# Which engine copies the second prompt tile's dense expert weights out of PSUM

## The reference

```
h = RMSNorm(x);  proj = h @ w_in                       # two attention branches, gates
x = x + w_out(sigmoid(gA) * (oA @ w_br_a) + sigmoid(gB) * (oB @ w_br_b))
x = x + PEER(RMSNorm(x))

PEER: q = h @ w_pq;  s1, s2 = q halves against 128 keys each
      top-16 of each half, top-16 of their 256 sums, for each of 8 heads
      e = i1 * 128 + i2;  g = softmax(top sums)         # 128 experts a token, of 16384
      a = gelu(u[e] . h);   y = sum over the 128 experts of g * a * v[e]
```

## Time and profile before

| | |
|---|---|
| Time, median of 3 runs | 1579.57 us (1575.74 to 1583.34) |
| Profiled execution | 1577.69 us, its span 1575.9 us |
| PE busy | 1167.5 us, 74% |
| DVE busy | 1035.7 us, 66% |
| POOL busy | 646.8 us, 41% |
| ACT busy | 291.7 us, 19% |
| mean granted TensorE clock | 0.816 of 2.4 GHz |

### The profile page before, as it was taken

One profiled execution on the slowest core, in us unless ns is written; L12 is line 12 of the kernel. 1 busy time (PEld: TensorE's weight loads), 2 busy tenths in 40 slices (PEclk: granted clock), 3 DMA queues, 4 the chain that ended last, 5 costly groups with the idle time before them and its releaser, 6 DMA issues.

```text
span 1575.9 us, 12501 instructions
## 1 busy us (share of the span) xinstructions
PE 1167.5 (74%) x4129; PEld 695.2 (44%) x4129; DVE 1035.7 (66%) x2220; ACT 291.7 (19%) x701; POOL 646.8 (41%) x565
## 2 busy tenths in 40 slices
PE   7999998975420683674586584027799999999998
PEld 3444444852110673673244374026544444444443
DVE  2436313579999878777447569999856566666664
ACT  2024501210000011111046441149600000000000
POOL 1110000333333757767324453445544454444451
PEclk9999999997755555555698777556799999999999
DMA  7654231684643988998987765656699999999996
GB/s 265 219 187 164 81 143 44 250 293 161 250 140 97 358 275 325 364 339 282 389 296 250 253 228 202 228 175 208 233 409 410 409 410 409 409 409 410 409 401 252
DMA packets 155361, 434.92 MB, mean 276 GB/s; under 512 B 14592, under 2 KB 36496, under 8 KB 155040
## 3 DMA queue, kind: packets, MB, share of 16 engines
q0 software_dynamic: 74688, 271.66, 46.8%
q1 hardware_dynamic: 80608, 162.45, 28.3%
HBM read 427.72 MB, written 6.34 MB: 275 GB/s over the span
## 4 chain that ended last, share of the span: by engine, by line
PE 56%; DVE 21%; DMA 9%; ACT 8%; issue 3%; POOL 3%; SPq 1%; DVEq 0%; ACTq 0%
PE wide L1189 28%; DVE rows_ring L1505 6%; PE accumB L873 5%; PE accumA L873 4%; DMA ring<-in_w_in 3%; DMA rows_ring<-in_peer_u,expert 3%; ACT hot L805 3%; POOL rows_ring L576 2%; PE wide L1079 2%; PE accumB L1101 2%; PE accumB L1135 2%; PE transB L849 2%; PE transB L1135 2%; PE wide L952 2%; PE wide L991 2%
## 5 line engine op out<-in xcount | busy, mean ns | idle before, releaser
L576 POOL DMA_INDIRECT rows_ring<-in_peer_u,expert x384 | 477.9, 1245 | 437.8 <-DVE dots L1505 351.0
L1505 DVE CUSTOM_DVE_ANT_0 rows_ring<-rows_ring,arena 128x1024 f32<-128x1024 f32 x384 | 458.6, 1223 | 125.4 <-DMA rows_ring<-in_peer_u,expert 123.0
L1189 PE MATMUL wide<-ring,arena 128*128 128x512 f32 x1024 | 439.7, 592 | 0.7 <-issue 0.7
L1189 PEld LDWEIGHTS wide<-ring,arena 128*128 128x128 f32 x1024 | 194.5, 190 | 245.3 <-issue 245.3
L1510 DVE SCALAR_TENSOR_TENSOR x<-rows_ring,dots,x 128x1024 f32<-128x1024 f32 x128 | 164.4, 1284 | 99.2 <-DMA rows_ring<-in_peer_v,expert 99.2
L576 POOL DMA_INDIRECT rows_ring<-in_peer_v,expert x128 | 127.1, 993 | 136.1 <-DVE x L1510 129.1
L849 PE MATMUL transB<-ident,arena 128*128 128x128 f32 x198 | 48.7, 389 | 126.8 <-DVE arena L1290 59.8
L873 PE MATMUL accumB<-ring,arena 128*128 128x512 f32 (+1 forms) x192 | 89.1, 622 | 56.9 <-ACT arena L651 50.0
L849 PEld LDWEIGHTS transB<-ident,arena 128*128 128x128 f32 x198 | 31.5, 195 | 141.3 <-DVE arena L1290 60.6
L873 PE MATMUL accumB<-arena 128*128 128x512 f32 x160 | 74.4, 620 | 23.9 <-ACT arena L651 12.3
L873 PEld LDWEIGHTS accumB<-ring,arena 128*128 128x128 f32 x192 | 40.0, 212 | 103.5 <-ACT arena L651 52.4
(11 more groups left out here) (218 smaller groups left out, 1418.0 us busy)
## 6 DMA issues: line engine op xcount, KB each, us to landing
ring<-in_peer_v SPq DMA_DIRECT2D x128, 512.0 KB, 6.8
ring<-in_w_in SPq DMA_DIRECT2D x10, 2048.0 KB, 10.2
arena<-in_w_in SPq DMA_DIRECT2D x10, 2048.0 KB, 8.8
ring<-in_w_pq SPq DMA_DIRECT2D x4, 2048.0 KB, 9.9
arena<-in_w_pq SPq DMA_DIRECT2D x4, 2048.0 KB, 8.9
arena<-in_w_out SPq DMA_DIRECT2D x3, 2048.0 KB, 10.3
rows_ring<-in_peer_u,expert POOLq DMA_INDIRECT x384, 6.8
arena<-in_w_br_a SPq DMA_DIRECT2D x2, 2048.0 KB, 7.6
```

The costliest lines, as they stand in the source:

```text
L576: pool.indirect_dma_start(rowbuf[:, n % ROWS, :], None, u_rows if n < U_ROWS else v_rows, index).then_inc(S(f"rows{n % ROWS}"), 16)
L1189: ins = pe.matmul(wide[:, 2 * t + half, :], dense[t][:, b, :], vblock[:, b % VBLOCKS, half * 512:half * 512 + 512], start=b == 0, stop=b = ...
L1505: v.tensor_tensor_reduce(row, row, h2[:, t, :], 1.0, 0.0, ALU.mult, ALU.add, dots[:, t, k:k + 1]).then_inc(S("row_used"), 1)
```

## The change

For tile 1 (`t == 1`) the copy out of PSUM leaves ScalarE's list and goes into VectorE's. VectorE copies group k = n-1 after the `hot1` of group n, behind a wait for `built` of group k; after the last `hot1` it copies group 30 and then group 31. ScalarE's waits ahead of tile 1's first copy go to VectorE with it, where two are added: that the router's scores were copied, and that tile 0's 32 copies are done. Tile 0 is as before.

```diff
                         act.wait_ge(S("state_stored"), 16 * 10)
-                    elif g == 0:
-
-                        act.wait_ge(S("routed"), 12)
-                        act.wait_ge(S("row_used"), SAMPLE * SLOTS)
-                        act.wait_ge(to(G1, "score_done"), 4)
-                    if g:
+                    if g and t == 0:
                         put(g - 1)
-                put(TGROUPS - 1)
+                if t == 0:
+                    put(TGROUPS - 1)
...
                     signal(ins, "hot1_ready")
+                    if t == 0:
+                        continue
+                    if g == 0:
+
+                        v.wait_ge(S("routed"), 12)
+                        v.wait_ge(S("row_used"), SAMPLE * SLOTS)
+                        v.wait_ge(to(G1, "score_done"), 4)
+                        v.wait_ge(to(G1, "router_copied"), 4)
+                        v.wait_ge(S("dense_put"), TGROUPS)
+                    for k in [g - 1] * (g > 0) + [g] * (g == TGROUPS - 1):
+                        v.wait_ge(S("built"), TGROUPS + k + 1)
+                        signal(v.tensor_copy(dense[t][:, :, k * TOKENS:k * TOKENS + TOKENS],
+                                             built[(k + 1) % 2][:, :].rearrange("p (n b) -> p b n", n=TOKENS)),
+                               "dense_put")
```

## The result

The changed kernel takes 1587.07 us (median of 20 runs, 1582.28 to 1593.15), the kernel before 1581.40 beside it (20 runs). The ratio is 1.0042, 95% interval 1.0030 to 1.0055: 4.7 to 8.7 us slower. Timed a second time, on another occasion, it is 1.0047 (1.0024 to 1.0069). The forecast was 1592 in a range of 1582 to 1600, so direction and range hold; but 0.42% lies under the 0.5% that I had named as the bound of "no change", a band to which I gave a chance of 0.15 only. And the size is about half of the forecast: 6.6 us by the ratio (5.7 between the medians), where the sum had 14.1.

What follows compares the result with a forecast made beforehand. ScalarE bounds tile 1's weight building, whose last copy gates the closing pass. Moving the copies makes steps 12.37 us instead of 10.30, +14.1 us: 1577.69 + 14.1 = 1591.8, said as 1592, range 1582 to 1600.

Steps and rivals of the forecast that it cites:

- no change: Whole kernel: a time within about 0.5%, 7.9 us, of the kernel before; chance of "same" 0.15.
- the sum: Tile 1's weight building: step period 12.37 us against 10.30, last copy done at 1144.6 against 1130.49, +14.1 us.
- The bound and the pass: Closing PE pass: waits only for tile 1's last dense-weight copy, starts near 1144.7, keeps its 439.7 us.
- The price of the copy: Tile 1's VectorE copies out of PSUM, 128x512 f32: 0.60 us each, 2.40 us a step.
- C: Rival on tile 1's copies: 0.35 us each on VectorE with fast builds, -2.4 us, 1575.3; chance 0.05.
- D: Rival on tile 1's copies: the PSUM source's stride makes each 1.2 us, about +24 us, 1602; chance 0.10.
- First builds slow: Tile 1's steps: the first build of each takes 2.05 us on PE, after about 4.7 us of rest.
- rival A: Tile 1's steps: the first build of each stays fast, period 11.86 us, +10.5 us, 1588.2; chance 0.25.
- All later builds slow: Tile 1's steps: builds behind the first run slow too, two slow ones in a row ending 1.71 us apart.
- Rows and gathers: Gathers land in time; four more rows behind the pass's start cost 8.2 us, 2.05 each, within 12.64 us of cover.
- rival B: Tile 1's steps: all builds fast, VectorE alone sets 11.27 us a step, +4.3 us, 1582.0; chance 0.10.

Runs made afterwards that it cites:

- the doubled copy: Changed kernel with each VectorE copy done a second time behind a wait for the first: 1603.33 us, ratio to the kernel before 1.0158.
- The two kernels with extra products: Kernel before and changed kernel, each with unused PE products after tile 1's builds: 1575.11 us (ratio 0.9973) and 1582.49 us (1.0029 to the kernel before).

## Why the prediction was right, and where it was not

*The bound and the pass: right.* The pass follows the last copy (1137.78 + 0.69, pass at 1138.57) and kept its 439.72 us.

*The price of the copy: right.* 0.60 us added, 0.685 to 0.69 alone, as the two-input row from PSUM; a cost of the stride doesn't show. That row could not decide it, though: two-input instructions out of SBUF add 0.60 for 128x512 too, so it doesn't tell what a one-input copy loses by reading PSUM. With C and D out by the copies themselves, the doubled copy confirms that VectorE pays for them. The Trainium skill's rule (VectorE: DVE Perf Modes, "Why PSUM operands drop a tier"), one element a cycle for f32 out of PSUM, agrees with these rows: an SBUF copy of that size would have been about half as long by the earlier trace rows.

*First builds slow: right,* eight of eight in the first trace and 32 of 32 in all four (2.04 or 2.05 us), where five of eight took 1.13 to 1.20 us before; that is rival A out. That the stretch grew by just A's +10.5 and that the time lies nearest to A's 1588.2 is luck. In the changed kernel the granted clock falls during the rest ahead of a step, here between the builds of 1064.40 and 1070.27 (columns as in the earlier trace rows):

```profile
1066.00:1068.00 2.00, 0.00 (x0) 0.00 (x0) 2.00 (x5) 1.97 (x6) 1.70 (x2) 1.00 0.00 0
1069.00:1070.00 1.00, 0.00 (x0) 0.00 (x0) 1.00 (x6) 0.00 (x0) 0.95 (x1) 0.50 0.83 307
```

The two kernels with extra products bear this out: with PE's rest filled, the clock of the stretch is 0.96. The Trainium skill's rule (TensorE: Matmul & The Clock Gate, Part 1) that activity lifts the clock agrees with that, 0.71 to 0.96 here.

The prediction's reading of the kernel before was weaker than it looked. There the first builds of tile 1 don't sort by the rest ahead of them: beside the very first (15.43 us of rest), two take 2.05 and 2.08 us after 1.62 and 1.78 us of rest (at 1089.95 and 1110.38), and the five of 1.13 to 1.20 us come after 1.67 to 2.47. They sort by the clock granted just ahead of them, 0.50 for the long builds and 1.00 for the short. And five short builds of eight is the most of four traces: 13 of 32 in all (1.13 to 1.33 us).

*All later builds slow: the step that was mis-sized.* "So I take the slow build for every first one, and also for those behind it": but the fourth ran fast in all steps and the third in half of them. The period is 84.64 / 7 = 12.09 us instead of 12.37, 2.0 us over seven, and the last step ends 0.5 us sooner (9.0 from its first hot1 to the last copy's end instead of 9.49). Together that is 96.1 predicted to last copy's end against 93.6 measured.

*The base was a short one.* The trace I summed against has a stretch of 82.05; the mean of four is 82.95. So +10.5 is the change's cost in the stretch, where the forecast had +14.1: 2.5 from the builds, 0.9 from the base, the rest the means.

*Rows and gathers: right in kind, too dear in size.* No row in the stretch waited for its gather. At the end VectorE still waited 8.57 us for PE, where 12.64 - 8.2 = 4.4 was forecast: the four rows more cost 4.1 us, about their own 1.15 each, and not 2.05, since seven rows behind the pass's start ran without waiting for a gather, where it was three before.

```profile
1578.31 2.36 DVE L1528 TENSOR_TENSOR x<-wide,x 128x1024 f32<-128x1024 f32 x2 [8.57 <-PE wide L1185]
```

*The chances: too sure.* Everything in the sum bore on a stretch of 82 us out of 1580, and the time outside it moves: the first hot1 of the changed kernel stands anywhere from 1044.8 to 1052.6. The range held since it reached down to rival B's 1582; the sum itself is 5 us over, and the kernel before, timed beside the changed one, came out 1.8 us above the 1579.57 that it started from. Of the 10.5 us in the traces, the two ratios show 6.6 and 7.4. Those 3 to 4 us stay open: the other runs have no trace.

## What to carry to other kernels

An engine that is on the chain in a stretch may still be the cheaper place for the work, if the one that would take it over has only little idle time there: add up the busy time of both in that window, not over the span (ScalarE 17 to 19%, VectorE 66%, and still: here 9.2 us a step on ScalarE against 11.1 on VectorE). Moving all of a job from one nearly full engine to another moves the bound; sharing it out, with the steps made fuller so that the row work goes where it has cover, and with PE's rest filled, gained 0.5% where the full move lost 0.4% (without the filling 0.2%, with no change in the interval; the parts of sharing and fuller steps are not told apart). And when a chain passes through short products on a mostly idle PE, look at the clock they run at: filling PE's rest gained 0.27% in the kernel before (interval 0.06 to 0.49%).

## What the runs showed of the hardware that I had not expected

VectorE's four 128x128 instructions take 1.02 us until a following copy starts, where four of eight in a row take 1.07. After eight 128x512 products (8.57 us, ending at 1043.43) PE idled and the granted clock was 1.00 in the window from 1044 to 1048, then 0.54 in the one from 1048 to 1050. And the start of a stretch that no edit touched differs by 7.7 us between traces of one kernel.
